# New start addresses for the on-chip tensors of a two-block transformer kernel: every fp32r matmul operand at a multiple of 512 bytes

## The chip, the cores and the metric

One core of one Trainium2 chip runs the whole kernel, all in 32-bit floats. The metric is the device time of one execution in microseconds (us). The time before is the median of three runs. The profile is one further execution, taken by the hardware profiler.

## The reference, cut to what matters

Two blocks over 512 tokens of width 1024. The first is feed-forward, token mixer (mLSTM and HGRN2 heads), feed-forward; the second has two layers of attention (neighbourhood, then differential), feed-forward and a gated projection. Nearly all of the arithmetic is matrix products of the activations with weights that are each used once:

```python
y = swiglu(y, ffn1_w_gate, ffn1_w_up, ffn1_w_down)        # 1024 -> 2816 -> 1024, first block, twice
p = y @ w_in                                               # 1024 -> 4104
return merged @ w_out                                      # 1024 -> 1024
qkv = h @ w_qkv                                            # 1024 -> 3072, in both layers
return (jax.nn.gelu(gate) * val) @ w_out                   # 1024 -> 2816 -> 1024, second block, in both layers
x = x + jax.nn.sigmoid(rms_norm(x, g) @ ple_w_gate) * (p @ ple_w_proj)
```

## The kernel before

Activations are held with features on the partitions and 512 tokens along the partition: `h`, and the split input of a product as `yh` and `yl` (`[128, 8, 512]` each; `hidh`, `hidl` with 22 such rows for the hidden layer; `moh`/`mol`, `oh`/`ol`, `gh`/`gl`, `ph`/`pl` for mixer output, attention output, gate and projection). A product is computed in three passes of fp32r matmuls (a 32-bit type that TensorE takes in one pass): high by high, low by high, high by low. SyncE loads weights into `raw` in units of 1 MB, ScalarE rounds one half of a unit into `wh` (L771), VectorE writes the remainder into `wl` (L1343), and TensorE multiplies. All of these matmuls have one line, L2044:

```python
def passes(bank, w_h, w_l, xh, xl, first, last, swap=False):
    for i, (w, x) in enumerate(((w_h, xh), (w_l, xh), (w_h, xl))):
        a, b = (x, w) if swap else (w, x)
        ins = nc.tensor.matmul(bank, a, b, start=first and i == 0, stop=last and i == 2)
```

The first operand is the stationary one (128 columns, 512 bytes of a partition), the second the moving one. As a rule the stationary operand is a piece of `wh` or `wl` and the moving one a row of 512 tokens, 2048 bytes. With `swap` (the values of the mixers) the stationary operand is a piece of `yh` or `yl` and the moving one is 256 columns of weights, two runs of 512 bytes. `gemm` runs eight of the three-pass steps for each tile of output, `opening` does the same for the first tiles of a stage, `beside_mixers` and `beside` deal such steps out between the small matmuls of the mixers. The mixers also have plain fp32 matmuls (`pair`, `att`, `PT` with `dv` at L2499, transposes against `ident` at L2488), and the norms have fp32 sums against `ones`. The one place outside L2044 with fp32r is L2479, the scores of the differential attention (`qkh`, `oh`, `ol`; 64 rows, two matmuls side by side).

The program is written with explicit semaphores. Order, waits and DMAs are in the code and do not follow from where a tensor lies.

Tensors are allocated one after the other in the order of the code; those opened in a `with ExitStack() as c:` block give their place back, so later ones overlie them (`hidh` and all tensors of the mixers and attention start at the same byte). The first tensor, `h`, starts at byte 16,512 of each partition in the compiled program, and each next address is the sum of the sizes before it. `raw`, `wh`, `wl`, `yh`, `yl` have sizes that are multiples of 512 bytes and so keep the remainder of `h`; `tmpB` (4224 bytes), `cst` (1280) and the small tensors change it.

| tensor | start before, byte | remainder by 512 | start after | remainder |
|---|---|---|---|---|
| `h`, `yh`, `yl` | 16512, 32896, 49280 | 128 | 17920, 34304, 50688 | 0 |
| `raw`, `wh`, `wl` | 65664, 82048, 98432 | 128 | 67072, 83456, 99840 | 0 |
| `ph`, `pl` (over `yh`) | 36992, 41088 | 128 | 38400, 42496 | 0 |
| `tmpA` | 114816 | 128 | 116224 | 0 |
| `tmpB` / `tmpC` | 118912 / 123136 | 128 / 256 | 130560 / 126464 | 0 / 0 |
| `acc`, `rstd` | 127232, 129280 | 256 | 120320, 122368 | 0 |
| `cst` (with `ident`) | 131328 | 256 | 16512 | 128 |
| `ones` | 133632 | 0 | 135808 | 128 |
| `hidh` and all that overlies it (`moh`, `oh`, `gh`, `qkh`, `PT`, `pair`, ...) | from 139008 | 256 | from 138752 | 0 |

Of the kernel before, what the change touches and what calls it, by code (L numbers as in the profile page):

```python
# [18 lines left out]
P = 128  # L19
D = 1024  # L20
S = 512
# [61 lines left out]
def build(nc, A, out):  # L83
    ctx = ExitStack()
    with ctx:
        def sb(name, shape, dt=F32, where=ctx):
            return where.enter_context(nc.sbuf_tensor(name, shape, dt))
# [2 lines left out]
            return ctx.enter_context(nc.semaphore(name))  # L90


        h = sb("h", [P, KT, S])
        with ExitStack() as c:
            yo_ffn = sb("yo_ffn", [P, KT, S], F32, c)
# [15 lines left out]
        wh = sb("wh", [P, 4, KT, P], F32R)  # L111
        wl = sb("wl", [P, 4, KT, P], F32R)
        A2 = sb("tmpA", [P, 2, S])
        with ExitStack() as c:
            ada_c = sb("ada_c", [P, UNIT], F32, c)[:, :]
        B2 = sb("tmpB", [P, 2, S + 16])
        C2 = sb("tmpC", [P, 2, S])
        acc = sb("acc", [P, S])
        R = sb("rstd", [P, S])
        cst = sb("cst", [P, 320])  # L120
        with ExitStack() as c:
            ada_row = sb("ada_row", [P, UC], F32, c)
        lev = sb("lev", [P, 8, P], U8)
        ones = sb("ones", [P, P])
        ms = sb("ms", [P, S])
        vec = sb("vec", [P, 448])
        small = sb("small", [64, 16])
        mod = sb("mod", [P, 80])
        coef = sb("coef", [P, 6, KT])
        lbc = sb("lbc", [P, 4, NH])  # L130
        sm = sb("sm", [P, 32])
        lamc = sb("lamc", [P, 16])
        t5 = sb("t5", [32, 16])
        silc = sb("silc", [P, 16])
        rcol = sb("rcol", [P, 16])
        uT = sm[:, 0:TT * NH]
        ident = cst[:, 0:P]
        namask = cst[:, 2 * P:2 * P + 64]
        staged = A2[:, :, :].rearrange("p a (b n) -> p (a b) n", b=2)
        av_last = C2[0:64, :, :].rearrange("p a s -> p (a s)")  # L140
        masks = B2[:, :, :].rearrange("p a s -> p (a s)")[:, 0:640]

# [325 lines left out]
        def evicted(eng, g):  # L468

            eng.wait_ge(gfree[BANK[g]], ORD[g] + 1)  # L470
# [35 lines left out]
        FULL = (2, 4)  # L506
        acc_hy = B2[:, 0, 0:S]
        acc_yy = B2[:, 1, 0:S]

        def root_place(e):  # L510
            return C2[:, 0, :] if e in FULL else R[:, :]

# [18 lines left out]
        def head_root(x):  # L531
            return R[:, :] if x < 2 * NH else B2[:, 0, 0:S]

# [95 lines left out]
        def _(pool):  # L629
# [5 lines left out]
            def add_squares(e, count):  # L635
                for k in range(count):
# [10 lines left out]
                    if k == 0 and e not in LATE:  # L647
                        nc.gpsimd.tensor_copy(acc[:, :], C2[:, n % 2, :]).then_inc(sq_acc, 1)
                    else:
                        nc.gpsimd.tensor_tensor(acc[:, :], acc[:, :], C2[:, n % 2, :], ALU.add)\  # L650
                            .then_inc(sq_acc, 1)
# [51 lines left out]
            for e, norm in enumerate(NORMS):  # L703
# [8 lines left out]
                if e == 3:  # L712
                    for n in range(NH * TT):
                        pool.wait_ge(wexp, n + 1)
                        w = C2[:, n % 2, 0:P]
                        nc.gpsimd.affine_select(out=w, in_=w, compare_op=ALU.is_ge, fill=0.0, base=0,
# [12 lines left out]
        def _(act):  # L729
# [43 lines left out]
            def square(e, k, src):  # L773
                n = SQ[e] + k
                if n >= 2:
                    act.wait_ge(sq_acc, n - 1)
                nc.scalar.activation(C2[:, n % 2, :], src, ACT.Square, scale=1.0 / 32.0).then_inc(sq_ready, 1)  # L777

            def log_and_exp():
                nc.scalar.preload_act_table_set("natural_log_exp_and_others")  # L780

            def rsqrt(to, of, bias, scale=1.0):
                if bias is None:
                    st.do(nc.scalar.activation(to, of, ACT.Ln, scale=scale))
                else:
                    st.do(nc.scalar.activation(to, of, ACT.Ln, bias=bias, scale=scale))
                return nc.scalar.activation(to, to, ACT.Exp, scale=-0.5)
# [15 lines left out]
            def pre_bias(e, first=None):  # L803
# [3 lines left out]
                for k in range(KT) if first is None else first:  # L807
                    n = KT * PRE[e] + k
                    act.wait_ge(t_ready, KT * (e // 2) + k + 1)
                    if k >= 2:  # L810
                        act.wait_ge(y_ready, n - 1)
                    st.do(nc.scalar.activation(B2[:, k % 2, 0:S], A2[:, k % 2, :], ACT.Identity,
                                               scale=scale[:, k:k + 1], bias=bias[:, k:k + 1]))
                    nc.scalar.activation(yh[:, k, :], B2[:, k % 2, 0:S], ACT.Copy).then_inc(yh_ready, 1)

# [8 lines left out]
            def out_tile(e, k, b, g, yo):  # L824
# [11 lines left out]
                if k == KT - 1:  # L836
                    act.wait_ge(most_mm, POST[e] + 1)
                to = acc_yy if k == 0 else A2[:, 1, :] if k < KT - 1 else acc[:, :]
                nc.scalar.activation(to, yo[:, k, :], ACT.Square, scale=1.0 / 32.0).then_inc(yy_ready, 1)

            def ffn(f, e):
                b0, g0, conv, hb = BB[f"ffn{f}"], TB[f"ffn{f}"], f >= 2, FT * f
                for j in range(J):
                    for i in range(2):
# [3 lines left out]
                        if not conv:  # L848
                            if j:
                                act.wait_ge(hid_ready, hb + 2 * j + i - 1)  # L850
                            nc.scalar.activation(A2[:, i, :], PS[BANK[g]][:, :], ACT.Silu).then_inc(gfree[BANK[g]], 1)
                    for i in range(2):
# [4 lines left out]
                        if conv:  # L857
                            act.wait_ge(conv_ready, FT * (f - 2) + 2 * j + i + 1)
                            if j:
                                act.wait_ge(hid_ready, hb + 2 * j + i - 1)  # L860
                            bias = vec[:, VOFF["fconv_b"] + FT * (f - 2):VOFF["fconv_b"] + FT * (f - 1)]
                            nc.scalar.activation(A2[:, i, :], C2[:, i, :], ACT.Gelu_apprx_tanh,
                                                 bias=bias[:, 2 * j + i:2 * j + i + 1]).then_inc(sg_ready, 1)
                        evicted(act, g)
                        nc.scalar.activation(hidh[:, 2 * j + i, :], A2[:, i, :], ACT.Copy).then_inc(hidh_ready, 1)  # L865
                log_and_exp()
# [47 lines left out]
            def mix():  # L914
# [68 lines left out]
                def finish(z, kind, x, f):  # L983
# [3 lines left out]
                    if kind == "M" and f == 0:  # L987
                        act.wait_ge(nd_mm, z + 1)
                        act.wait_ge(ho2_ready, z)
                        nc.scalar.activation(R[:, :], G[3][:, :], ACT.Square, scale=EPS ** 0.5).then_inc(em_ready, 1)  # L990
                    if f == 1:
                        act.wait_ge(ho_ready, z + 1)
                        nc.scalar.activation(acc[:, :], o, ACT.Square).then_inc(hsq, 1)
                    if f == 2:
                        act.wait_ge(hmm, z + 1)
                        if z:
                            act.wait_ge(ho2_ready, z)
                        rsqrt(R[:, :], X[0][:, :], lamc[:, 4:5] if kind == "H" else None, 1.0 / DH)\
                            .then_inc(hr_ready, 1)
# [268 lines left out]
        def _(dve):  # L1268
# [103 lines left out]
            def residual(e, k, yo):  # L1372
                st.do(nc.vector.tensor_tensor(yo[:, k, :], yo[:, k, :], R[:, :], ALU.mult))
                st.do(nc.vector.tensor_tensor(h[:, k, :], h[:, k, :], yo[:, k, :], ALU.add))
# [21 lines left out]
            def join_sums(e):  # L1396
                dve.wait_ge(sums_mm, POST[e] + 1)
                x = acc[:, :]
                st.do(nc.vector.tensor_tensor(x, X[3][:, :], R[:, :], ALU.mult))
                st.do(nc.vector.scalar_tensor_tensor(x, X[2][:, :], 2.0, x, ALU.mult, ALU.add))  # L1400
# [1268 lines left out]
```

## Time and profile before

| | |
|---|---|
| median of 3 runs | 2623.47 us (2622.88 to 2624.31) |
| span of the profiled execution | 2619.6 us |
| TensorE matmuls busy | 2494.6 us, 11538 instructions |
| TensorE weight loads busy | 1977.7 us, 11538 instructions |
| VectorE / ScalarE / GpSimd busy | 1523.7 / 1008.7 / 154.3 us |
| mean granted TensorE clock | 0.98 of full |

The span is what lies between the first and the last instruction; the runs' median is 3.9 us above it. [...]

### The profile page before, as it was taken

The page shows a single profiled execution, that of the slowest core. Times are in us where ns is not written, and L with a number is a line of the kernel's source. Part 1 is how long each engine was busy: PE and PEld are TensorE (multiplying, and loading weights), DVE is VectorE, ACT ScalarE, POOL GpSimd, SP SyncE. Part 2 cuts the span into 40 slices and gives each one's busy share as a digit, 9 for nine tenths or more (in the row PEclk, how much of TensorE's full clock was granted, in tenths as well). Part 3 has the DMA queues.
Part 4 walks back from the last instruction along what each step waited for, and adds up shares of the span by engine and source line. Part 5 has one row for each costly group of instructions (what it writes and reads, how often), then busy time and mean ns, then how long its engine had stood idle before and what let it go on. Part 6 is the DMA issues. An engine that isn't in the chain of part 4 may idle for free.

```text
span 2619.6 us, 29183 instructions
## 1 busy us (share of the span) xinstructions
PE 2494.6 (95%) x11538; PEld 1977.7 (75%) x11538; DVE 1523.7 (58%) x2379; ACT 1008.7 (39%) x1547; POOL 154.3 (6%) x166
## 2 busy tenths in 40 slices
PE   7999998989987999998999999999999999999998
PEld 4878876867766888886877688887777767888876
DVE  5876436677647333336654855534866668555445
ACT  4222234444545322223444433333545554333333
POOL 0000111000010000010101000001100010000100
PEclk9999999999999999999999999999999999999999
DMA  9555427422212333222321222222232212222321
GB/s 365 170 193 193 143 89 157 105 53 54 60 42 67 111 98 98 93 89 73 99 79 57 95 98 97 93 97 93 81 102 70 79 39 91 97 97 93 104 86 65
DMA packets 233704, 265.90 MB, mean 102 GB/s; under 512 B 8376, under 2 KB 222008, under 8 KB 233568
## 3 DMA queue, kind: packets, MB, share of 16 engines
q1 hardware_dynamic: 220704, 223.39, 28.1%
q0 software_dynamic: 11088, 37.46, 4.4%
q10 hardware_dynamic: 1776, 3.18, 0.3%
q8 instruction: 92, 1.51, 0.2%
q14 instruction: 44, 0.36, 0.0%
HBM read 259.78 MB, written 10.75 MB: 103 GB/s over the span
## 4 chain that ended last, share of the span: by engine, by line
PE 62%; DVE 6%; issue 3%; ACT 3%; POOL 0%; DMA 0%; POOLq 0%; ACTq 0%; DVEq 0%
PE G L2044 54%; DVE wl L1343 1%; PE X L2044 1%; PE G L2499 1%; PE X L2479 1%; ACT yh L820 1%; DVE yl L1369 1%; DVE h L1432 1%; PE G L2437 1%; DVE tmpA L1384 1%; PE X L2404 1%; PE X L2488 1%; ACT wh L771 1%; PE X L2418 0%; DVE nbias L1821 0%
## 5 line engine op out<-in xcount | busy, mean ns | idle before, releaser
L1343 DVE TENSOR_TENSOR wl<-raw,wh 128x1024 fp32r<-128x1024 f32 (+1 forms) x398 | 474.8, 1199 | 695.3 <-ACT wh L771 695.0
L2044 PE MATMUL G<-yh,wh 128*128 128x512 f32 x1864 | 754.2, 405 | 49.9 <-DVE yl L1361 15.7
L2044 PE MATMUL G<-yl,wh 128*128 128x512 f32 x1864 | 732.7, 393 | 0.0
L2044 PE MATMUL G<-yh,wl 128*128 128x512 f32 x1864 | 732.3, 393 | 0.0
L771 ACT ACTIVATE wh<-raw 128x1024 fp32r<-128x1024 f32 (+1 forms) x398 | 410.0, 1037 | 821.0 <-PE G L2044 803.0
L2044 PEld LDWEIGHTS G<-yh,wh 128*128 128x128 f32 x1864 | 353.9, 190 | 150.1 <-issue 31.5
L2044 PEld LDWEIGHTS G<-yl,wh 128*128 128x128 f32 x1864 | 353.5, 190 | 76.1
L2044 PEld LDWEIGHTS G<-yh,wl 128*128 128x128 f32 x1864 | 354.0, 190 | 71.6 <-issue 2.4
L2044 PE MATMUL G<-hidh,wh 128*128 128x512 f32 x704 | 279.7, 397 | 0.0
L2044 PE MATMUL G<-hidl,wh 128*128 128x512 f32 x704 | 278.0, 395 | 0.0
L2044 PE MATMUL G<-hidh,wl 128*128 128x512 f32 x704 | 278.0, 395 | 0.0
L2044 PEld LDWEIGHTS G<-hidh,wl 128*128 128x128 f32 x704 | 132.2, 188 | 32.7 <-issue 1.0
L2044 PEld LDWEIGHTS G<-hidh,wh 128*128 128x128 f32 x704 | 132.2, 188 | 32.6 <-issue 1.0
L2044 PEld LDWEIGHTS G<-hidl,wh 128*128 128x128 f32 x704 | 132.2, 188 | 31.9
L650 POOL TENSOR_TENSOR acc<-acc,tmpC 128x512 f32<-128x512 f32 x51 | 86.2, 1691 | 953.3 <-ACT tmpC L777 953.3
L865 ACT ACTIVATE hidh<-tmpA 128x512 fp32r<-128x512 f32 x88 | 55.6, 632 | 207.4 <-DVE tmpA L1487 207.4
L2044 PE MATMUL G<-wh,yh 128*128 128x256 f32 x384 | 113.7, 296 | 3.6 <-DVE mqk L1549 2.0
L2044 PE MATMUL G<-wh,yl 128*128 128x256 f32 x384 | 109.2, 284 | 0.0
L2044 PE MATMUL G<-wl,yh 128*128 128x256 f32 x384 | 109.2, 284 | 0.0
L1490 DVE TENSOR_TENSOR hidl<-tmpA,hidh 128x512 fp32r<-128x512 f32 x88 | 61.0, 693 | 61.5 <-ACT hidh L865 61.5
L2044 PEld LDWEIGHTS G<-wh,yh 128*128 128x128 f32 x384 | 74.1, 193 | 8.9 <-issue 7.0
L2044 PEld LDWEIGHTS G<-wl,yh 128*128 128x128 f32 x384 | 74.2, 193 | 0.4 <-issue 0.2
(351 smaller groups left out, 3001.3 us busy)
## 6 DMA issues: line engine op xcount, KB each, us to landing
raw<-in_ffn_w_in SPq DMA_DIRECT2D x44, 1024.0 KB, 5.0
raw<-in_ffn_w_gate SPq DMA_DIRECT2D x22, 1024.0 KB, 5.4
raw<-in_ffn_w_up SPq DMA_DIRECT2D x22, 1024.0 KB, 5.3
ada_c<-in_ada_w POOLq DMA_DIRECT2D x20, 1024.0 KB, 5.6
raw<-in_ffn_w_down SPq DMA_DIRECT2D x16, 1024.0 KB, 5.1
raw<-in_w_in SPq DMA_DIRECT2D x16, 1024.0 KB, 9.5
raw<-in_ffn_w_out SPq DMA_DIRECT2D x16, 1024.0 KB, 5.3
ada_z<-in_ada_w SPq DMA_DIRECT2D x14, 1024.0 KB, 10.9
```

The costliest lines, as they stand in the source:

```text
L650: nc.gpsimd.tensor_tensor(acc[:, :], acc[:, :], C2[:, n % 2, :], ALU.add)\
L771: nc.scalar.activation(place(wh), src, ACT.Copy).then_inc(hi, 1)
L820: nc.scalar.activation(to, of, ACT.Identity, scale=pre_scale(e)[0][:, k:k + 1]).then_inc(yh_ready, 1)
L865: nc.scalar.activation(hidh[:, 2 * j + i, :], A2[:, i, :], ACT.Copy).then_inc(hidh_ready, 1)
L1343: nc.vector.tensor_tensor(place(wl), src, f32(place(wh)), ALU.subtract).then_inc(lo, 1)
L1369: nc.vector.scalar_tensor_tensor(to, of, pre_scale(e)[0][:, k:k + 1], upper, ALU.mult, ALU.subtract)\
L1384: hy = nc.vector.scalar_tensor_tensor(to, h[:, k, :], 1.0 / D, yo[:, k, :], ALU.mult, ALU.mult)
L1432: nc.vector.tensor_tensor(h[:, k, :], h[:, k, :], yo[:, k, :], ALU.add).then_inc(h_ready, 1)
L1490: nc.vector.tensor_tensor(hidl[:, 2 * j + i, :], A2[:, i, :], f32(hidh[:, 2 * j + i, :]), ALU.subtract).then_inc(hid_ready, 1)
L2044: ins = nc.tensor.matmul(bank, a, b, start=first and i == 0, stop=last and i == 2)
L2404: nc.tensor.matmul(X[m][:, UC * i:UC * i + w], aq[r, p, qt * P:(qt + 1) * P], ak[r, p, k0:k0 + w], start=True, stop=True).then_inc(na_s, 1)
L2437: ins = nc.tensor.matmul(G[2][r, to], v, x, start=part == 0, stop=part == 4)
```

## The change

No instruction is added, taken away or moved. Three things change in the allocations: `cst` and `sm` go in front of `h`; `acc`, `rstd` and `ms` go ahead of `tmpC` and `tmpB`, whose order is turned; and four small tensors (`small`, `t5`, `silc`, `rcol`) become unused columns of `mod`, `lamc`, `sm` and `lbc`. The starts that follow stand in the table above.

```diff
+        cst = sb("cst", [P, 320])
+        sm = sb("sm", [P, 32])
         h = sb("h", [P, KT, S])
...
         A2 = sb("tmpA", [P, 2, S])
+        acc = sb("acc", [P, S])
+        R = sb("rstd", [P, S])
+        ms = sb("ms", [P, S])
         with ExitStack() as c:
             ada_c = sb("ada_c", [P, UNIT], F32, c)[:, :]
+        C2 = sb("tmpC", [P, 2, S])
         B2 = sb("tmpB", [P, 2, S + 16])
-        C2 = sb("tmpC", [P, 2, S])
-        acc = sb("acc", [P, S])
-        R = sb("rstd", [P, S])
-        cst = sb("cst", [P, 320])
         with ExitStack() as c:
             ada_row = sb("ada_row", [P, UC], F32, c)
         lev = sb("lev", [P, 8, P], U8)
         ones = sb("ones", [P, P])
-        ms = sb("ms", [P, S])
         vec = sb("vec", [P, 448])
-        small = sb("small", [64, 16])
         mod = sb("mod", [P, 80])
+        small = mod[0:64, 72:80]
         coef = sb("coef", [P, 6, KT])
         lbc = sb("lbc", [P, 4, NH])
-        sm = sb("sm", [P, 32])
         lamc = sb("lamc", [P, 16])
-        t5 = sb("t5", [32, 16])
-        silc = sb("silc", [P, 16])
-        rcol = sb("rcol", [P, 16])
+        t5 = lamc[0:32, 8:16]
+        silc = sm[:, 24:32]
+        rcol = lbc[:, 3, :]
```

## Rows read from the trace of the kernel before

**Rows 1.** The page: span, and busy time of each engine.

```profile
span 2619.6 us, 29183 instructions
...
PE 2494.6 (95%) x11538; PEld 1977.7 (75%) x11538; DVE 1523.7 (58%) x2379; ACT 1008.7 (39%) x1547; POOL 154.3 (6%) x166
```

**Rows 2.** TensorE's groups by line and shape: count, busy us, mean ns.

```profile
L2044 PE MATMUL G<-yh,wh 128*128 128x512 f32 x1864 | 754.2, 405 | 49.9 <-DVE yl L1361 15.7 <-DVE yl L1369 10.7 <-issue 9.6
...
L2044 PE MATMUL G<-hidh,wh 128*128 128x512 f32 x704 | 279.7, 397 | 0.0
...
L2044 PE MATMUL G<-wh,yh 128*128 128x256 f32 x384 | 113.7, 296 | 3.6 <-DVE mqk L1549 2.0 <-DVE aq L1762 1.7
...
L2044 PE MATMUL G<-gh,wh 128*128 128x512 f32 x128 | 52.9, 414 | 9.0 <-DVE wl L1343 4.7 <-DVE gl L1369 4.3
...
L2044 PE MATMUL G<-oh,wh 128*128 128x512 f32 x96 | 41.7, 435 | 0.8 <-issue 0.8
```

**Rows 3.** Waits in total, longest first: us, times, longest us.

```profile
ACT wh L771 <- PE G L2044: 803.0, 252, 9.4
DVE wl L1343 <- ACT wh L771: 695.0, 275, 8.5
```

**Rows 4.** VectorE's line L1343 by shape: count, busy us, mean ns.

```profile
L1343 DVE TENSOR_TENSOR wl<-raw,wh 128x1024 fp32r<-128x1024 f32 x365 | 444.1, 1223 | 602.9 <-ACT wh L771 602.7
```

**Rows 5.** TensorE in unbroken stretches: busy us (matmuls), clock, DMA share, GB/s.

```profile
855.00:955.00 100.00, 100.00 (x443) 1.00 0.32 103
...
1077.00:1127.00 50.00, 50.00 (x216) 1.00 0.29 95
...
1510.00:1610.00 100.00, 100.00 (x443) 1.00 0.29 95
...
2430.00:2480.00 50.00, 50.00 (x216) 1.00 0.27 87
```

**Rows 6.** Timeline of TensorE, swapped matmuls at full clock: start us, us.

```profile
1969.17 0.28 PE L2044 MATMUL G<-wh,yh 128*128 128x256 f32 x1
1969.29 0.28 PE L2044 MATMUL G<-wl,yh 128*128 128x256 f32 x1
1969.41 0.28 PE L2044 MATMUL G<-wh,yl 128*128 128x256 f32 x1
```

**Rows 7.** Timeline of TensorE, a plain fp32 product of two passes, then scores.

```profile
2012.80 3.59 PE L2499 MATMUL G<-PT,dv 128*128 128x512 f32 x8
2016.32 0.51 PE L2479 MATMUL X<-qkh 64*128 64x512 f32 x2
2016.66 0.40 PE L2479 MATMUL X<-qkh,oh 64*128 64x512 f32 x2
2016.89 0.39 PE L2479 MATMUL X<-ol,qkh 64*128 64x512 f32 x2
```

**Rows 8.** TensorE inside a half-clock stretch: busy us (matmuls), granted clock.

```profile
536.00:541.00 5.00, 4.03 (x8) 0.50 0.00 0
```

**Rows 9.** Timeline of TensorE in the same stretch.

```profile
540.12 0.63 PE L2044 MATMUL G<-yh,wh 128*128 128x512 f32 x1
540.55 0.63 PE L2044 MATMUL G<-yh,wl 128*128 128x512 f32 x1
540.97 0.59 PE L2044 MATMUL G<-yl,wh 128*128 128x512 f32 x1
```

**Rows 10.** The three mixer stages: busy us of PE, PEld, DVE, ACT, POOL.

```profile
447.00:818.00 371.00, 332.92 (x1674) 263.75 (x1672) 248.04 (x391) 167.70 (x277) 16.53 (x23) 0.97 0.30 68
...
1197.00:1455.00 258.00, 241.40 (x1387) 192.26 (x1387) 154.70 (x359) 111.51 (x245) 25.86 (x35) 0.97 0.27 80
...
1905.00:2165.00 260.00, 255.41 (x1323) 188.80 (x1322) 168.65 (x357) 142.26 (x273) 11.92 (x12) 0.99 0.23 75
```

**Rows 11.** VectorE's line L1369: min/median/max ns.

```profile
L1369 DVE SCALAR_TENSOR_TENSOR yl<-h,vec,yh x32: 737/753/1787, 1194.5 to 2193.7; 128x512 fp32r<-128x512 f32 x32
L1369 DVE SCALAR_TENSOR_TENSOR gl<-h,vec,gh x16: 750/752/753, 1836.1 to 2574.2; 128x512 fp32r<-128x512 f32 x16
```

**Rows 12.** ScalarE's line L820: min/median/max ns.

```profile
L820 ACT ACTIVATE yh<-h,vec x32: 709/724/1338, 1193.3 to 2192.9; 128x512 fp32r<-128x512 f32 x32
L820 ACT ACTIVATE gh<-h,vec x16: 714/723/725, 1835.3 to 2573.4; 128x512 fp32r<-128x512 f32 x16
```

## Prediction

> **What bounds the kernel now.** I read the page's busy times first. TensorE's matmuls cover 95% of the 2619.6 us, no other engine more than 58% [rows 1], so the cost of one matmul in a stream sets the time. The waits say the same from the other side: ScalarE waits 803 us in total for TensorE before it may overwrite `wh`, and VectorE 695 us for ScalarE [rows 3]. The weight path is well ahead.
>
> Then the groups by shape, for the counts [rows 2]. The three passes have equal counts. Moving operand `yh` or `yl`: 3 x 1864 = 5592 matmuls of 512 columns. Hidden layer: 3 x 704 = 2112. Gate: 3 x 128 = 384. Attention output: 3 x 96 = 288 in the G banks, and 3 x 32 = 96 in X banks, counted from the code (four output tiles of eight there). Mixer output, counted likewise: 192. Projection (`ph`, `pl`): 3 x 32 = 96. Swapped, 256 columns: 3 x 384 = 1152. By the table of starts, 5592 + 96 = 5688 have the moving operand at remainder 128 and 2112 + 384 + 384 + 192 = 3072 at remainder 256; every stationary operand of L2044 is at 128 today.
>
> The third view is what one costs. In a stretch that TensorE fills without a break, the last matmul reaches about 0.39 us past its start, so the distance between starts is (stretch + 0.39) / count. For `yh`/`yl`: 100.39 / 443 = 226.6 ns, in two stages alike. For `hidh`/`hidl`: 50.39 / 216 = 233.3 ns, again in two stages [rows 5]. Swapped: 120 ns [rows 6]. The reader is to see two things. The same line with the same shapes costs 6.7 ns more where the moving tensor starts at remainder 256 than where it starts at 128. And all are above what the columns need at 2.4 GHz, 512 / 2.4 = 213.3 ns and 256 / 2.4 = 106.7 ns: by 13.3 ns at 128 whatever the width, by 20.0 ns at 256.
>
> **What could be taken off.** A plain fp32 matmul shows how little is needed beyond the columns. Eight `PT`,`dv` entries take 3.59 us from first start to last end [rows 7]; without the duration of the last, 0.59 us, seven distances make 3.00 us, 428 to 429 ns each, which is 2 x 213.3 + 2.5. That type passes its columns at half the rate, and its operands lie at remainder 256, so at half the rate the start costs nothing. The half-clock stretch agrees: at 0.50 granted (1.2 GHz) [rows 8] the fp32r matmuls start 0.43 us apart [rows 9], 512 / 1.2 = 427 and no more. So what is lost is lost in feeding a column each 0.42 ns, not in issue or semaphores. [...]
>
> **The change part by part.** It removes and adds no instruction, wait or DMA, so every price is a change in the duration of what is there.
>
> 1. fp32r operands go from 128 and 256 to remainder 0. The trace has no fp32r matmul at 0, so both sides are bounded. Below: the fp32 excess of 2.5 ns, so 215.8 ns (and 109.2 for 256 columns). From the excesses of 32 ticks of 2.4 GHz at 128 and 48 at 256, a straight line through the moving start leaves 16 ticks at 0: 220.0 ns. Above: the dearest row, 233.3 ns, if 0 is as bad as 256. I take 215.8: 13.3 ns at 128 are 16 ticks of 1.2 GHz, which is 128 bytes at 8 bytes a tick, the very rate at which 2048 bytes take 213.3 ns; bytes ahead of the start, down to a 512-byte boundary, would be fetched for nothing, and at 0 there are none. That 256 costs 24 such ticks and not 32 fits if the mean of both operands' starts counts, (256 + 128) / 2 = 192 bytes. It is an inference from two points.
>  Savings: 10.9 ns at 128, 17.5 at 256, 10.8 for a swapped one. Feed-forward, projection and gate are straight streams. Each feed-forward has 44 tiles x 8 x 3 = 1056 at 128 and 528 at 256; four make 4224 x 10.9 = 46.0 and 2112 x 17.5 = 37.0 us; projection and gate 96 x 10.9 + 384 x 17.5 = 7.8. Together 90.8; about 3% of time is at half clock or behind waits at the start of stages, where nothing is saved: 88 us.
>  The mixer and attention stages have the rest: 1368 x 10.9 + 576 x 17.5 + 1152 x 10.8 = 37.4 us. There TensorE is busy 829.7 of 889 us [rows 10], but part of the steps only fill time until VectorE or ScalarE has made the next small operand, and saved time there becomes a wait. I take two thirds, 25 us; the bounds are a third and all.
> 2. Plain fp32 matmuls: `PT`, `pair`, `tmpC`, `acc` go to 0, `ones` from 0 to 128, `cst` from 256 to 128. By [rows 7] a start at 256 costs nothing at this rate: 0. What hides it is the half rate of columns; bound, if each of the 1434 (11538 less 9912 of L2044 and 192 of L2479) lost 6.7 ns: 10 us.
> 3. VectorE and ScalarE: the same lines write `yl` and `gl`, `yh` and `gh`, at remainders 128 and 256, in medians of 753 and 752, 724 and 723 ns [rows 11, 12]. 0, and no less: neither engine sets the end.
> 4. DMAs: same number and sizes, landing under other work at 30% of the queues' time [rows 5]. 0.
> 5. The four folded tensors: same instructions, other columns. 0.
>
> Sum: 88 + 25 = 113 us. On the profiled span: 2619.6 - 113 = 2506.6, and 3.9 us more for the runs' median: about 2511 us. If the weight path had to follow a faster TensorE: a half-unit needs 1.22 us of VectorE [rows 4] against 24 x 215.8 ns = 5.2 us of TensorE, and both engines of that path wait hundreds of us [rows 3], so it stays hidden.
>
> **The rivals.**
> - *Half the gain (2546 us).* The straight line holds, 220.0 ns: 6.7 ns saved at 128 and 13.3 at 256. Straight streams 4320 x 6.7 + 2496 x 13.3 = 62.1, less 3%, 60; mixers 24.5 x 2/3 = 16. For it: fewest assumptions. Against: it leaves an unexplained 16 ticks that plain fp32 lacks.
> - *Only the difference of the two starts counts (2605 us).* Moving and stationary operand at equal remainders cost 226.7, unequal ones 233.3; after the change all are equal. Then only the 3072 gain 6.7 ns: 2496 x 6.7 = 16.6 and 576 x 6.7 x 2/3 = 2.6, 19 us. Against it: the score matmuls of L2479 have both operands at 256, and the pairs start 0.34 us apart once and 0.23 once [rows 7]; neither is below 226.7 ns, but pairs are not single matmuls, so this is weak.
> - *No change (2623 us).* All operands at 256 lie above byte 139,008 and all at 128 below 114,816; the 6.7 ns may belong to the place in memory, and the 13.3 ns to fp32r itself. No row separates these. [...]
> - *Slower (2663 us).* The remainder that matters is that by 256: then 128 is the better and 256, like 0, the dearer start, as when two operands that both begin on a boundary ask for the same memory at once. Everything goes to 233.3 ns: 4320 x 6.7 x 0.97 = 28, and (1368 + 1152) x 6.7 x 2/3 = 11, +39 us. The rows at 128 and 256 allow it. It decides from a start distance of 229 ns, the present mean over the 8760.
>
> **How the numbers follow.** The full gain 0.43, half 0.13, the difference 0.09, no change 0.20, slower 0.15. The range from 2490 (all 37.4 us of the mixers counted, and a little) to 2626 us leaves out the slower case alone. The likeliest case's own range is 2494 to 2524. A measurement of this kernel can tell 0.2%, 5 us, from no change: faster 0.65, same 0.20, slower 0.15.
>
> **What would show it.** In stretches like those of [rows 5], 465 matmuls in 100 us instead of 443, and 233 instead of 216 in 50 us; swapped ones 0.11 us apart; `PT`,`dv` still 3.59 us; L1369 and L820 unchanged; ScalarE's wait for TensorE shorter by some 100 us. If `hidh` falls to 227 ns and `yh` stays, the third case is right; if `yh` rises to 233, the last. Wrong without either: start distances fall as I say but gaps before L2044 grow in the mixers by more than 12 us.

## Result and the profile after

| | before | after |
|---|---|---|
| median | 2623.36 us (4 runs, 2622.88 to 2624.31) | 2606.55 us (4 runs, 2602.72 to 2608.31) |
| span of the profiled execution | 2619.6 us | 2601.0 us |
| ratio | | 0.9938, 95% interval [0.9925, 0.9951] |

The kernel became 0.6% faster, 17 us. The predicted time was 2511 us. The result lies inside the range, at the time of the third case, 2605 us, which had been given a chance of 0.09; the range covered it together with most other rivals, so that lying inside it says little. The two programs have the same instructions on every engine, under the new names of the folded tensors.

The page of the kernel after, answering to [rows 1]:

```profile
span 2601.0 us, 29183 instructions
...
PE 2476.1 (95%) x11538; PEld 1975.7 (76%) x11538; DVE 1522.8 (59%) x2379; ACT 1008.6 (39%) x1547; POOL 154.7 (6%) x166
```

TensorE's busy time fell by 18.5 us, the span by 18.6; VectorE and ScalarE stand still. TensorE in unbroken stretches, as in [rows 5] (busy us, matmuls, granted clock, DMA share, GB/s). The first and third stretch multiply `yh`/`yl`, the second and fourth `hidh`/`hidl`:

```profile
855.00:955.00 100.00, 100.00 (x443) 1.00 0.30 95
1070.00:1120.00 50.00, 50.00 (x222) 1.00 0.29 95
...
1500.00:1600.00 100.00, 100.00 (x443) 1.00 0.30 95
...
2415.00:2465.00 50.00, 50.00 (x222) 1.00 0.30 98
```

What a matmul costs is read as the distance from its start to the next one's, for the entries overlap: those of 256 columns last 0.28 us and start 0.12 us apart [rows 6], the last one of 512 columns in a stretch ends 0.39 us after its start. The reader is to see that 443 stayed 443, (100 + 0.39) / 443 = 226.6 ns, although `yh` went from remainder 128 to 0, and that 216 became 222, (50 + 0.39) / 222 = 227.0 ns instead of 233.3. The whole gain lies in the tensors that were dearer; all now cost what the cheaper ones always did. The groups by shape (count, busy us, mean ns), as in [rows 2], say the same, and `PT`,`dv` shows that plain fp32 did not move:

```profile
L2044 PE MATMUL G<-yh,wh 128*128 128x512 f32 x1864 | 754.4, 405 | 49.7 <-DVE yl L1361 15.7 <-DVE yl L1369 10.6 <-issue 9.6
...
L2044 PE MATMUL G<-hidh,wh 128*128 128x512 f32 x704 | 275.6, 392 | 0.0
...
L2044 PE MATMUL G<-wh,yh 128*128 128x256 f32 x384 | 113.7, 296 | 3.3 <-DVE mqk L1549 2.0 <-DVE aq L1762 1.4
...
L2499 PE MATMUL G<-PT,dv 128*128 128x512 f32 x64 | 28.9, 594 | 0.7 <-ACT PT L1161 0.7
```

The waits in total, as in [rows 3]: ScalarE waits 17 us less for a TensorE that is faster by as much.

```profile
ACT wh L771 <- PE G L2044: 785.8, 250, 9.3
DVE wl L1343 <- ACT wh L771: 680.4, 272, 8.5
```

**Where the 18.6 us of the two spans lie.** From the first matmul of one stage to the first of the next, by their start times in the two traces: the four down projections are shorter by 3.1, 3.4, 3.4 and 3.4 us, 13.3 together (528 matmuls x 6.6 ns = 3.5 each), the two gates by 0.8 and 0.9. The stretches of `yh` and of the mixers before the four down projections changed by -0.2 (a saving), -0.4, -3.4 and +0.3 us. The 3.4 us are no matter of starts. At 1334 us the kernel after is 7.4 us ahead at the same matmul, at 1364 us already 10.2 and soon 10.5 us. Between the two lies a stretch of 6.8 us at half clock, in the middle of neighbourhood attention, that this execution of the kernel after did not have. Windows of TensorE from the same matmul on, before and then after:

```profile
1357.00:1360.00 3.00, 3.00 (x17) 0.53 0.22 53
1360.00:1364.00 4.00, 4.00 (x13) 0.50 0.65 226
```

```profile
1350.00:1353.00 3.00, 3.00 (x21) 1.00 0.37 79
1353.00:1357.00 4.00, 4.00 (x23) 1.00 0.58 203
```

In the 17 us ahead of these windows TensorE was busy for 14.8 us both times, so the traces do not show why the clock fell in one and not in the other. All half-clock stretches together amount to 86.6 us of the trace before and 78.4 us of the trace after, and to other sums in other layouts (79.9 and 102.2 us in the second and fourth experiment). They go with what differs from run to run: of the four runs of the kernel after, the one of 2602.72 us had a mean granted clock of 0.985 and the three of 2606 to 2608 us had 0.983. About 15 us are left to the change itself, more or less by the runs: the medians differ by 16.8 us here and by 19.1 in the last experiment.

### The profile page after: what moved, and what is told of

Read it like the earlier page. It is cut to its first block, busy times and chain, and to the rows that moved or that the text cites. A ratio compares the mean times of both kernels' runs of the same rounds, so it can differ in the third digit from the quotient of the medians.

```text
span 2601.0 us, 29183 instructions
## 1 busy us (share of the span) xinstructions
PE 2476.1 (95%) x11538; PEld 1975.7 (76%) x11538; DVE 1522.8 (59%) x2379; ACT 1008.6 (39%) x1547; POOL 154.7 (6%) x166
## 2 busy tenths in 40 slices
DMA packets 233704, 265.90 MB, mean 102 GB/s; under 512 B 8376, under 2 KB 222008, under 8 KB 233568
## 4 chain that ended last, share of the span: by engine, by line
PE 62%; DVE 6%; issue 3%; ACT 3%; POOL 0%; DMA 0%; POOLq 0%; ACTq 0%; DVEq 0%
PE G L2044 54%; DVE wl L1343 1%; PE X L2044 1%; PE G L2499 1%; PE X L2479 1%; ACT yh L820 1%; DVE yl L1369 1%; DVE h L1432 1%; PE G L2437 1%; PE X L2404 1%; PE X L2488 1%; DVE tmpA L1384 1%; ACT wh L771 0%; PE X L2418 0%; DVE nbias L1821 0%
## 5 line engine op out<-in xcount | busy, mean ns | idle before, releaser
L1343 DVE TENSOR_TENSOR wl<-raw,wh 128x1024 fp32r<-128x1024 f32 (+1 forms) x398 | 474.5, 1199 | 680.9 <-ACT wh L771 680.4
```

The lines of the kernel that those rows point to most:

```text
L1343: nc.vector.tensor_tensor(place(wl), src, f32(place(wh)), ALU.subtract).then_inc(lo, 1)
```

## The experiments

These theories were set against each other after the result. A: what counts is the difference between the starts of the moving and the stationary operand. B: what counts is where the moving operand starts, 0 and 128 being cheap and 256 dear. And for the 13.3 ns that all fp32r matmuls of 512 columns have above 213.3: a fixed price of the type (F), or the load of the next stationary operand, whose entries (188 ns each in the third bench) lie beside the matmuls. The 213.3 ns are half of what 512 columns take at 0.50 granted, 0.43 us [rows 8, 9] and 426 to 427 ns by the start times. The widths agree: at full clock and equal starts 256 columns more take 226.7 - 119.7 = 107.0 ns in the first bench, 0.418 ns a column. So a column is reckoned here at 0.417 ns at full clock and 0.833 at half; the prediction writes this as 2.4 and 1.2 GHz.

**1. A bench of starts.** In place of the computation:

```diff
+            for m in (0, 128, 256, 384):
+                for w in (0, 128, 256, 384):
+                    configs.append((mv[m], st[w], S, P))
...
+            for c, (m, w, n, cols) in enumerate(configs):
+                for i in range(NREP):
+                    ins = nc.tensor.matmul(G[c % 4][0:cols, 0:n], w[:, i % 8, 0:cols], m[:, i % 2, 0:n],
+                                           start=i == 0, stop=i == NREP - 1)
```

> A bench that leaves the whole computation out and writes zeros: 48 matmuls in a row for each pair of operand starts, nothing else running. The distance between two starts is what is read. Theory A, the difference of the two starts counts: fp32r, 512 columns, 227 ns for every pair with equal remainders (0/0, 128/128, 256/256, 384/384) and about 233 ns for unequal ones. Theory B, the moving operand's own start counts: 227 ns with the moving operand at 0 or 128 and 233 ns at 256 or 384, whatever the stationary start. For the 13.3 ns that all have in common: if the load of the next stationary operand takes them (128 columns of 4 bytes, one tick of 2.4 GHz for every 16 bytes), 64 stationary columns give 220 ns and 32 give 217; if they are a fixed price of the fp32r type, both stay at 227. bf16 operands: 216 ns in both. Plain fp32: 429 ns.

The timeline of TensorE (start us, duration of 48 matmuls in us). Tensors are named for the remainder of their start by 512; the last matmul is 0.39 us long, so the distance is (duration - 0.39) / 47:

```profile
42.72 11.32 PE L107 MATMUL G<-mov_zero,sta_onetwentyeight 128*128 128x512 f32 x48
53.88 11.05 PE L107 MATMUL G<-mov_zero,sta_twofiftysix 128*128 128x512 f32 x48
...
75.92 11.30 PE L107 MATMUL G<-mov_onetwentyeight,sta_zero 128*128 128x512 f32 x48
87.06 11.05 PE L107 MATMUL G<-mov_onetwentyeight,sta_onetwentyeight 128*128 128x512 f32 x48
97.95 11.32 PE L107 MATMUL G<-mov_onetwentyeight,sta_twofiftysix 128*128 128x512 f32 x48
109.11 11.05 PE L107 MATMUL G<-mov_onetwentyeight,sta_threeeightyfour 128*128 128x512 f32 x48
120.00 11.05 PE L107 MATMUL G<-mov_twofiftysix,sta_zero 128*128 128x512 f32 x48
...
142.04 11.05 PE L107 MATMUL G<-mov_twofiftysix,sta_twofiftysix 128*128 128x512 f32 x48
...
208.16 11.37 PE L107 MATMUL G<-mov_thirtytwo,sta_zero 128*128 128x512 f32 x48
219.37 11.15 PE L107 MATMUL G<-mov_sixtyfour,sta_zero 128*128 128x512 f32 x48
...
406.19 10.31 PE L107 MATMUL G<-bmov_zero,bsta_zero 128*128 128x512 bf16 x47
...
488.61 41.36 PE L107 MATMUL G<-fmov_twofiftysix,fsta_zero 128*128 128x512 f32 x96
```

Every pair with a difference of 0 or 256 bytes takes 11.05 us, 226.7 to 226.8 ns each, at whatever place (the very first case, 0/0, took 14.07 us: it began with starts 427 ns apart, and its median is 227); every pair 128 or 384 apart takes 11.30 to 11.32 us, 232.2 to 232.4 ns by the start times. With the moving operand 32 bytes ahead it is 233.5, 64 ahead 228.8; with the stationary one 64 ahead 233.4. A was expected to count by 512; it counts by 256. B fails: the moving operand at 256 is cheap beside a stationary one at 0 or 256. bf16 has 215.8 ns, and plain fp32 429 with starts 256 apart, as expected; it was not tried 128 apart. The 429 ns are the distance of its entries in the trace, and a plain fp32 matmul has two of them (x96 for the 48 matmuls of the code), where an fp32r matmul has one (x48 for 48): fp32r is taken in one pass, plain fp32 in two. `PT`,`dv` is counted likewise, eight entries for the four matmuls of one product [rows 7]. With the moving tensor above byte 139,264 and the weights at 128, the starts 0, 128 and 256 gave 232.5, 227.7 and 233.3 ns, which is the same picture. For the 13.3 ns neither theory's number came: at equal starts 64 stationary columns cost 230.0 ns and 32 columns 231.8. Fewer columns are not cheaper, which speaks against the load as I had priced it.

The same bench holds two answers that I had not asked for (means of 47 start distances, starts equal and then 128 bytes apart). The price of the difference depends on the width of the moving operand: 226.7 and 232.4 ns for 512 columns, 173.5 and 176.1 for 384, 119.7 and 118.6 for 256. And it is gone with few stationary columns: 230.0 and 229.8 ns with 64, 231.8 and 230.6 with 32.

**2. Hidden layer 128 bytes up.** The kernel after, with

```diff
+        sb("ahead", [P, 32])
         with ExitStack() as c:
             hidh = sb("hidh", [P, FT, S], F32R, c)
```

> The changed kernel with the hidden layer and all that overlies it moved up by 128 bytes: moving operand at remainder 128, weights at 0. Theory A (difference): 233 ns between starts in the down projections, 2606 + 19 = 2625 us. Theory B (moving start alone, 128 as good as 0): 227 ns and 2606 us.

Windows of TensorE in this run, `yh` and then `hidh`:

```profile
855.00:955.00 100.00, 100.00 (x443) 1.00 0.31 97
1080.00:1130.00 50.00, 50.00 (x216) 1.00 0.28 93
```

216 again: 233.3 ns, with a moving operand at 128, the start that was cheap for `yh`. The median was 2618.58 us against 2623.7 of before, 0.9988 [0.9977, 0.9999]. A holds. The time is 6 us below the 2625 that I gave; the down projections last as long as before to 0.1 us, and the 4.6 us between its span (2615.0) and that of before lie in stages where the two starts kept their difference. There 6.7 us less ran at half clock, which is worth 3.4 us.

**3. Everything 256 bytes up.** The kernel after, with

```diff
+        sb("ahead", [P, 64])
         cst = sb("cst", [P, 320])
         sm = sb("sm", [P, 32])
```

> The changed kernel with everything moved up by 256 bytes, so that all fp32r operands start at remainder 256 and none at a multiple of 512. Theory A (difference): nothing changes, 227 ns everywhere, 2606 us. Theory B (256 is a dear start for the moving operand): 233 ns everywhere, 2606 + 19 + 39 = 2664 us.

Windows at `yh` and `hidh`:

```profile
855.00:955.00 100.00, 100.00 (x443) 1.00 0.31 96
1080.00:1130.00 50.00, 50.00 (x222) 1.00 0.29 95
```

2603.18 us, 0.9922 [0.9905, 0.9939]. No fp32r operand that the four feed-forwards read starts at a multiple of 512, and the gain is all there: the four down projections last 124.1 and three times 121.7 us, as in the kernel after.

**4. Only the small tensors folded, and 128 bytes ahead of the hidden layer.** The kernel before, with

```diff
-        small = sb("small", [64, 16])
         mod = sb("mod", [P, 80])
+        small = mod[0:64, 72:80]
...
-        t5 = sb("t5", [32, 16])
-        silc = sb("silc", [P, 16])
-        rcol = sb("rcol", [P, 16])
+        t5 = lamc[0:32, 8:16]
+        silc = sm[:, 24:32]
+        rcol = lbc[:, 3, :]
...
+        sb("ahead", [P, 32])
         with ExitStack() as c:
             hidh = sb("hidh", [P, FT, S], F32R, c)
```

> The kernel before with only the four small tensors folded away and 128 bytes put ahead of the hidden layer: all operands at remainder 128, order of the tensors as before. Both theories: 227 ns in the down projections, 2606 us, so that neither the multiple of 512 nor the new order is needed. If the multiple of 512 itself matters: 2623 us.

2607.23 us, 0.9933 [0.9918, 0.9947]; `hidh` counts 223 in 50 us. Neither the multiple of 512 nor the new order of the tensors is needed. Fold and pad together move the hidden layer down by 128 bytes, from 139,008 to 138,880.

**5. A second bench**, for other differences and for the 13.3 ns:

```diff
+            run([(row(mv[0]), zs)], banks=2)
+            run([(row(mv[0]), lambda i: st[0][:, 0, 0:P])])
+            run([(lambda i: mv[0][:, 0, 0:S], piece(st[0]))])
...
+            run([(zm, zs), (row(bm), piece(bs))], fresh=True)
```

> A second bench without the computation, 48 matmuls in a row for each case, all fp32r with 512 columns unless said. From the first bench: equal starts 226.7 ns, starts 128 bytes apart 232.4, 256 apart 226.7 again, so the difference counts and repeats after 256 bytes. [...] Theory F (the 13.3 ns above 213.3 are a fixed price of an fp32r matmul): the fp32r one by turns with bf16 stays at 227 ns with either start. [...]

Its tensors did not all start where their names say: `mov_zero` with `sta_zero` costs 233.3 ns here and cost 226.7 in the first bench. If every allocation is rounded up to 32 bytes, `sta_zero` lay at 32, `mov_ninetysix` at 128, `mov_onesixty` at 192, `sta_ninetysix` at 128, `sta_onesixty` at 192. The differences are then 96, 160, -32, -128 and -192 (256 - 192 = 64 by the remainder of 256) bytes for the five rows, and at these differences the third bench found the same costs to 0.3 ns (233.6, 234.1, 233.2, 232.5 and 228.8). The rows (start us, duration of 48):

```profile
32.57 11.38 PE L84 MATMUL G<-mov_ninetysix,sta_zero 128*128 128x512 f32 x48
43.78 11.41 PE L84 MATMUL G<-mov_onesixty,sta_zero 128*128 128x512 f32 x48
...
66.23 11.36 PE L84 MATMUL G<-mov_zero,sta_zero 128*128 128x512 f32 x48
77.42 11.31 PE L84 MATMUL G<-mov_zero,sta_ninetysix 128*128 128x512 f32 x48
88.57 11.16 PE L84 MATMUL G<-mov_zero,sta_onesixty 128*128 128x512 f32 x48
...
144.35 33.76 PE L84 MATMUL G<-mov_zero,sta_zero 128*128 128x512 f32 x144
```

By the start times 233.6, 234.2, 233.3, 232.2 and 229.1 ns: nothing is below 226.7, and a difference of 64 is again the mildest of the bad ones. The last row holds the three cases with two banks by turns, one stationary piece and one moving row: (33.76 - 0.39) / 143 = 233.4 ns, the same as without, at this difference of -32 bytes. At that difference 320 columns cost 146.7 ns and 448 columns 203.4, 13.4 and 16.7 more than their columns' 133.3 and 186.7, against 20 for 512: here too the difference costs less with a narrower operand. 112, 96 and 80 stationary columns cost 233.3, 228.9 and 233.4 ns, in no order. Alternating with bf16, a pair took 463 ns where the two fp32r operands were -32 bytes apart and 460 where they were 128 apart. I had expected from theory A that the fp32r matmul would fall to bf16's 216 ns there, 432 a pair; that did not come. The third bench takes this up.

**6. The mirror of the kernel before.** The fourth kernel, with

```diff
+        sb("before_weights", [P, 32])
         wh = sb("wh", [P, 4, KT, P], F32R)
```

> The small tensors folded, weights moved to remainder 256, hidden layer and all that overlies it at 256 too, yh and yl left at 128: the mirror of the kernel before. Theory A (difference): 232 to 233 ns between starts for yh and yl (5688 matmuls dearer by 6 ns, those in straight streams 4320 x 6 = 26 us, the rest by two thirds 5 us), 227 ns for hidh and hidl; 2606 + 31 = 2637 us. Theory B (moving operand at 256 is dear, at 128 cheap): the kernel before, 2623 us, with hidh at 233 and yh at 227.

Weights and hidden layer are at 256 now, `yh` at 128. Windows at `yh` and `hidh`:

```profile
870.00:970.00 100.00, 100.00 (x430) 1.00 0.31 95
1110.00:1160.00 50.00, 50.00 (x222) 1.00 0.29 95
```

The two have changed places: `yh` costs 100.39 / 430 = 233.5 ns and `hidh` 227.0, with not one byte of `yh` moved. 2629.12 us against 2620.47, 1.0039 [1.0025, 1.0053]. I had expected 2637, too much. Against the kernel after, the `yh` stretches of the last three feed-forwards are longer by 6.8, 5.5 and 5.5 us and that of the first by about 2, some 20 where I had put 26. The swapped matmuls have their starts 128 bytes apart now and did not get dearer (median 119 instead of 120 ns between starts), as the first bench shows for 256 columns.

**7. Hidden layer 256 bytes up.** The kernel after, with

```diff
+        sb("ahead", [P, 64])
         with ExitStack() as c:
             hidh = sb("hidh", [P, FT, S], F32R, c)
```

> The changed kernel with the hidden layer and all that overlies it at remainder 256, weights at 0. If the difference counts by its remainder by 256: 227 ns in the down projections and 2606 us, so that 512 is more than is needed. If by its remainder by 512: 233 ns and 2623 us.

2603.76 us, 0.9936 [0.9921, 0.9951]; `hidh` counts 222 in 50 us (1080 to 1130). 256 is enough in the kernel too.

**8. A third bench**, with finer shifts of one moving and one stationary tensor:

```diff
+            for e in (0, 1, 2, 4, 8, 12, 16, 20, 24, 32, 40, 48, 56, 64, 96, 128):
+                run(e)
+            for e in (4, 8, 16, 32, 64):
+                run(0, ww=e)
+            for e in (8, 16, 32):
+                run(e, ww=e)
+            for n in (64, 128, 192, 256, 384):
+                run(0, n=n)
+            run(0, k=64)
+            run(32, k=64)
...
+            run(0, turns=(0, 1))
...
+            run(0, turns=(1, 1, 1, 0))
```

> A third bench without the computation: two rows of moving operand and eight stationary pieces whose own distances are multiples of 256 bytes, so that the difference of starts is the same in all 48 matmuls of a case (in the second bench allocations were rounded up to 32 bytes and some cases mixed two differences). Difference theory: 226.7 ns at 0, 256 and 512 bytes, dearer between, with no case below 226.7; moving both starts by the same amount leaves 226.7. Widths 64 to 384 at equal starts: columns / 2.4 + 13.3 ns where the type runs at full rate. The 13.3 ns: if it is a fixed price of fp32r, one fp32r matmul among three bf16 (215.8 ns alone) adds 11 ns to the four; if it is the load of an fp32r stationary operand beside a full-rate moving one, it is gone there. 64 rows, two row halves by turns: per pair 227 ns at equal starts, 233 at 128 bytes.

The mean distances, from the trace's start times (moving operand ahead by bytes): 0: 226.7 (after the first starts of the bench, 427 ns apart); 4: 236.6; 8: 233.1; 16: 231.7; 32: 233.3; 48: 233.2; 64: 228.8; 80: 231.1; 96: 233.6; 128: 233.4; 160: 234.1; 192: 233.2; 224: 233.1; 256: 226.8; 384: 233.2; 512: 227.0. With the stationary operand ahead by 16 bytes it is 226.7, by 32 already 233.2 and by 128 232.5. Both ahead by 32, 64 or 128: 227.2, 227.2, 227.6. Nothing is below 226.7. With 64 rows and two halves by turns a pair costs 227 ns at equal starts and 233 at 128 bytes, as expected.

Widths: 256 and 384 columns at equal starts cost 119.9 and 173.5, their columns and 13.2 to 13.5. The narrower cases need a look at the clock. Windows of TensorE over the cases with 64 and 128 columns, then the end of that with 192 (busy us, matmuls, granted clock, DMA share, GB/s):

```profile
278.50:283.50 5.00, 5.00 (x47) 1.00 0.00 0
284.00:293.70 9.70, 9.70 (x48) 0.50 0.01 2
298.00:301.00 3.00, 3.00 (x29) 1.00 0.00 0
```

At full clock the matmuls of 64 columns start 112 ns apart, and those of 192 columns do too. The clock was at half over all of the 128-column case, which took 213.3 ns, and over the first 17 matmuls of 192 columns, which took 213.3 as well. 213.3 ns is what 256 columns take at half clock, half of the 427 for 512. So with 128 stationary columns the matmuls of fewer than 256 moving columns took nearly as long as one of 256, at either clock.

The mixture of the types (start us, us):

```profile
333.69 0.39 PE L84 MATMUL G<-bmov,bsta 128*128 128x512 bf16 x1
333.73 0.58 PE L84 MATMUL G<-mov,sta 128*128 128x512 f32 x1
334.15 0.39 PE L84 MATMUL G<-bmov,bsta 128*128 128x512 bf16 x1
334.19 0.58 PE L84 MATMUL G<-mov,sta 128*128 128x512 f32 x1
```

A pair takes 0.46 us, more than the 215.8 + 226.7 = 442.5 ns of the two alone. The change of type has a price of its own, about 17 ns a pair, and it covers what the case was to show. One fp32r among three bf16, at full clock throughout, repeats every 897 ns. F had put this at 874 (four times 215.8, and 11) and the load at 863; both miss, and what lies above can be the change of type again. F is neither shown nor refuted.

**9. The kernel after once more**, beside its kernel before on one chip.

> The changed kernel once more, beside its kernel before on one chip: 226.7 ns between starts everywhere and a ratio of 0.993, as for the three layouts with equal remainders by 256 (0.9922, 0.9933, 0.9936). If the multiple of 512 gave anything beyond them, the ratio would be below 0.992.

2602.18 us against 2621.27, 0.9928 [0.9915, 0.9942]; its windows count 443 in 100 us of `yh` and 222 in 50 us of `hidh`. With 0.9922, 0.9933 and 0.9936 for the three layouts that keep differences of 0 or 256 without starts of 0, the multiple of 512 adds nothing that can be measured.

## Why the prediction was wrong, point by point

- *What bounds the kernel.* Right: the span shrank by what TensorE's matmuls shrank by.
- *Step 1, fp32r operands to remainder 0.* This is the step that failed. It took the 13.3 ns at remainder 128 for bytes fetched ahead of the start, and so saw 215.8 ns at 0. Measured at 0: 226.6 ns. No run shows such a fetch, nor a term of 8 bytes a tick; it was an estimate fitted to two points. The 13.3 ns don't depend on a start that both operands share (both at 0, 128, 256 or 384: 226.7 to 226.8), and the 6.7 ns more of `hidh` came from its distance of 128 bytes to the weights. Two points, 128/128 and 256/128, were read as a row of moving starts while the stationary one stood at 128 in both; they fit a difference as well. The formula with the mean of both starts, made to fit the second point, gave the confidence and had no other support. The rows that seemed to show that a start costs nothing at half the rate, `PT` with `dv` [rows 7] and `yh` with `wh` at half clock [rows 9], have both operands at one remainder, so they had no difference to show. Rows that have one say the same, though: the gate's matmuls of the kernel before (256 against 128) start 0.43 us apart at half clock, and the fp32 matmuls of `cst` and `pb` (128 columns), whose starts went from equal to 128 bytes apart by the change, stayed at 109 ns.
- *Its sum.* The term for `yh`/`yl` (46.0 us) and the one for swapped matmuls measured nothing; the one for the hidden layer, 37.0 us, measured 13.3; projection and gate, 7.8, measured 1.7; the mixers, 25, nothing that can be told.
- *The third case, the difference.* It was right in mechanism, except that the remainder is by 256 and not by 512, and in price: 16.6 us for the streams against 15.0 measured (13.3 and 1.7). Its 2.6 us for the mixers were not there: the stretches with mixers stood still to 0.4 us once the half-clock stretch is set aside. Their output products did get cheaper (medians of 232 and then 227 ns between starts, 0.6 us for each of the three), and about 0.4 us of each was lost again in the gap before the sum of squares that follows. The objection that I raised against it, the score pairs of [rows 7], was an argument from rows not comparable with full-height matmuls.
- *No change.* The place in memory is refuted by the bench and by the sixth experiment. For fp32r with 512 columns the starts decide, 226.8 against 232.4 ns. For bf16 no start made a difference here (215.8 and 215.7 ns), nor for the plain fp32 matmuls whose difference changed, which have 128 columns; plain fp32 with 512 columns was tried at differences of 0 and 256 only.
- *Slower.* 256 as the dear start is refuted by the third experiment. But its sign lay near: had the moves put `yh` and the weights 128 bytes apart, the result would have been like the sixth kernel's, 1.0039.
- *Steps 2 to 5.* Right: `PT`,`dv` 594 ns as before; L1369 has medians of 753 and 751 ns, L820 724 and 724, against [rows 11, 12]; the DMAs move 233,704 packets and 265.90 MB both times.

What makes the difference dear was not shown. What was measured of it: the price depends on both starts (226.7 to 226.8 ns at 0/0, 128/128, 256/256 and 384/384, 232.2 to 232.4 at 128/0, 0/128 and 256/128); it appears at full clock and not at half, where `gh` with `wh` and `wl`, 128 apart, start 0.43 us apart like `yh` with `wh`; with 64 or 32 stationary columns it is gone (229.8 and 230.6 ns 128 apart, 230.0 and 231.8 at equal starts). bf16 has none of it: 215.8 ns at 0/0, and 215.7 ns at 256/128, from the row of 10.52 us, in which the record of one of the 48 matmuls is missing. No run took the load of the next stationary operand away, so its part is not shown. Open also is what the 13.3 ns are: not the start, not the width from 256 to 512 columns, not the bank, not the repetition of a piece, and not in proportion to the stationary columns.

## What to carry to other kernels

For streams of fp32r matmuls with 512 moving columns these runs speak for keeping moving and stationary tensors at the same remainder by 256 bytes, and every slice of them at multiples of 256; one odd-sized tensor between them cost 6.6 ns, 3%, of each matmul at full clock here (233.3 against 226.7 ns). A shift of the hidden layer by 128 bytes did what the new layout did (the fourth experiment). A rate read at two places where two things differ at once supports two laws: before taking the larger gain, look for the pair of rows that holds one of them still, and where there is none, give the laws like chances.

## What the runs showed of the hardware that I had not expected

- The difference counts by 256 bytes, not evenly. With the moving operand ahead it costs 6.6 ns at 32 bytes, 2.1 at 64, 5.7 to 6.7 at 128 and 9.9 at 4; 16 bytes are free on one side (stationary ahead) and cost 5.0 ns on the other.
- The narrower the moving operand, the less the difference of 128 bytes costs: 5.7 ns at 512 columns, 2.6 at 384, and at 256 it is 1.1 ns cheaper than none. With 64 or 32 stationary columns it costs nothing.
- fp32r with 64 and with 192 moving columns starts every 112 ns at full clock, little below the 119.9 ns of 256 columns; at half clock 128 and 192 columns both take 213.3 ns. All of these have 128 stationary columns.
- fp32r and bf16 matmuls by turns cost 460 ns a pair, 17 ns more than the two kinds alone.
